# Attention heads taken in pairs: transposed together, scored as 64-row products, gated together

## What is computed

```python
h = jnp.einsum('bnd,de->bne', x, w_in)
qa, ka, va, ga, qb, kb, vb, gb = jnp.split(h, IN_SPLITS, axis=-1)
qa, ka = _rope(qa), _rope(ka)                        # 8 heads of 64
out_a = _dilated_attention(qa, ka, va) * silu(ga)
qb = _axial_rope(_rms_norm_heads(qb, q_norm))        # 8 query heads
kb = _axial_rope(_rms_norm_heads(kb, k_norm))        # 2 key and value heads
out_b = _gqa_attention(qb, kb, vb) * silu(gb)
f = concat(out_a, out_b) @ w_out
y = layer_norm(ALPHA * x + f)
```

## Time and profile before

| | us |
|---|---|
| median of 3 runs | 475.74 |
| lowest, highest | 475.21, 476.89 |
| the profiled execution, first to last instruction | 474.6 |
| TensorE busy in it | 438.0 |
| VectorE, ScalarE, GpSimd busy | 301.4, 230.7, 248.1 |

### The profile page before, as it was taken

How to read it: one execution, slowest core, us unless ns; L and a number is a source line. 1 busy time by engine, 2 the same in 40 slices (tenths; PEclk the granted TensorE clock), 3 DMA queues, 4 the chain that set the end, 5 groups by cost and what they waited for, 6 DMA issues and landing times.

```text
span 474.6 us, 8965 instructions
## 1 busy us (share of the span) xinstructions
PE 438.0 (92%) x3292; PEld 413.2 (87%) x3292; DVE 301.4 (64%) x826; ACT 230.7 (49%) x519; POOL 248.1 (52%) x340
## 2 busy tenths in 40 slices
PE   1999979998899999999999999999999789999990
PEld 1999969987799999998899999999888678999990
DVE  1543675339987788664577877855586777433664
ACT  3332113335456565666565565655675876121222
POOL 1126953795554746334346565653543773454664
PEclk9999989999899999999999999999999989999997
DMA  6611212110200101102010010110200136231222
GB/s 237 255 45 52 71 35 74 39 46 23 68 23 23 46 23 36 56 24 66 14 54 23 24 46 24 40 51 23 68 1 23 44 111 245 88 95 42 78 100 89
DMA packets 23291, 30.00 MB, mean 63 GB/s; under 512 B 1872, under 2 KB 19408, under 8 KB 23248
## 3 DMA queue, kind: packets, MB, share of 16 engines
q1 hardware_dynamic: 22816, 29.30, 19.0%
q10 hardware_dynamic: 432, 0.13, 0.1%
HBM read 26.28 MB, written 3.15 MB: 62 GB/s over the span
## 4 chain that ended last, share of the span: by engine, by line
PE 66%; POOL 10%; DVE 10%; issue 7%; ACT 3%; DMA 2%; SPq 1%; ACTq 0%; DVEq 0%; POOLq 0%
PE bank L504 15%; PE bank L505 15%; PE bank L506 15%; PE bank L465 9%; PE bank L593 6%; POOL scr L1062 3%; DVE prob L870 2%; PE bank L551 2%; PE bank L552 2%; DMA h<-x_prompt 2%; DVE tmp_s L796 1%; POOL tanh L1048 1%; ACT prob L707 1%; DVE p_lo L878 1%; POOL w_lo L1032 1%
## 5 line engine op out<-in xcount | busy, mean ns | idle before, releaser
L504 PE MATMUL bank<-w_hi,t_lo 128*128 128x256 f32 x576 | 168.2, 292 | 1.9 <-DVE nmax L870 0.8
L506 PE MATMUL bank<-w_hi,t_hi 128*128 128x256 f32 x576 | 164.0, 285 | 0.0
L505 PE MATMUL bank<-w_lo,t_hi 128*128 128x256 f32 x576 | 163.9, 285 | 0.0
L504 PEld LDWEIGHTS bank<-w_hi,t_lo 128*128 128x128 f32 x576 | 111.5, 194 | 3.1 <-DVE nmax L870 1.0
L505 PEld LDWEIGHTS bank<-w_lo,t_hi 128*128 128x128 f32 x576 | 111.6, 194 | 0.1
L506 PEld LDWEIGHTS bank<-w_hi,t_hi 128*128 128x128 f32 x576 | 111.3, 193 | 0.0
L1032 POOL TENSOR_TENSOR w_lo<-raw,w_hi 128x512 fp32r<-128x512 f32 x52 | 67.2, 1302 | 59.2 <-ACT w_hi L659 59.1
L1113 POOL TENSOR_SCALAR prob<-prob,den 128x512 f32<-128x512 f32 (+1 forms) x96 | 60.5, 635 | 68.6 <-DVE den L899 68.5
L707 ACT ACTIVATE prob<-prob,nmax 128x512 f32<-128x512 f32 (+1 forms) x96 | 62.3, 649 | 54.1 <-DVE nmax L870 53.6
L878 DVE TENSOR_TENSOR p_lo<-bank,p_hi 128x512 fp32r<-128x512 f32 x80 | 54.8, 685 | 3.0 <-ACT p_hi L716 2.2
L659 ACT ACTIVATE w_hi<-raw 128x512 fp32r<-128x512 f32 x62 | 37.6, 622 | 34.6 <-DMA raw<-w_in 17.4
(11 more groups left out here) (97 smaller groups left out, 784.3 us busy)
## 6 DMA issues: line engine op xcount, KB each, us to landing
raw<-w_in SPq DMA_DIRECT2D x50, 256.0 KB, 2.8
raw<-w_out SPq DMA_DIRECT2D x16, 256.0 KB, 2.9
h<-x_prompt SPq DMA_DIRECT2D x7, 512.0 KB, 6.8
h<-x_sample SPq DMA_DIRECT2D x4, 512.0 KB, 9.6
y_prompt<-h SPq DMA_DIRECT2D x8, 256.0 KB, 2.1
y_sample<-h SPq DMA_DIRECT2D x4, 256.0 KB, 2.1
cst<-consts SPq DMA_DIRECT2D x1, 960.0 KB, 9.5
h<-x_prompt SPq DMA_DIRECT2D x2, 256.0 KB, 3.8
```

Source lines behind the costliest of these rows:

```text
L504: nc.tensor.matmul(out, a_lo, b_hi, start=(m == 0), stop=False)
L505: nc.tensor.matmul(out, a_hi, b_lo, start=False, stop=False)
L506: ins = nc.tensor.matmul(out, a_hi, b_hi, start=False, stop=(m == KT - 1))
```

## The change

Two neighbouring heads make a pair, 8 pairs with 5 steps each (w, 40 steps), and v = 2w + s counts the units as before, s being the head of the pair.

- Queries and keys of a pair lie side by side in 128 columns, so a batch transposes both heads at once and head s lands on rows 64s to 64s + 63. hi and lo get tensors of their own (`q_hi`, `q_lo`). `double_keys` and `k_two` go. For B, where both heads of a pair use one key head, the first key batch is copied to both row halves for both key heads (`twice`): four copies and four subtractions.
- Scores of a step are three rounds, lo x hi, hi x lo, hi x hi, and in each round a 64-row product for either head, on its row half, into its own bank.
- `LAG` becomes one step. Both masks of a step come first on VectorE; probability copies and exponentials alternate on ScalarE.
- Sums of the values get a bank for each head; the second is the one that the batches are transposed into, with waits both ways (`mixed` ahead of a batch, `t_lo_done` ahead of the second head's sums). Both heads are multiplied by the gate in one instruction of 128 partitions.
- The first key and value columns and rotation tables share space with the gates, and values of A get two more places in the space of B's queries.
- The schedules of items, splits and early output products are written anew for steps; six instead of four slices of the first output chunk lie inside the loop.

Its core; of the loops only the new lines stand here:

```diff
-LAG = 3
-STEPS = NU + LAG + 1
-BESIDE = ((0, 5), (3, 8), (55, 44), (62, 50), (65, 52), (72, 54))
-SPLIT_STEPS = (73, 75, 77, 79, 80, 81, 82)
-WIDE_AT = {76: ((0, (0, 1)),), 78: ((1, (0, 1)),), 80: ((2, (0, 1)), (0, (2, 3))), 81: ((1, (2, 3)),),
-           82: ((3, (0, 1)), (2, (2, 3))), 83: ((3, (2, 3)),)}
+LAG = 1
+STEPS = NW + LAG + 1
+BESIDE = ((0, 5), (2, 9), (26, 44), (30, 50), (33, 52), (36, 54))
+SPLIT_AT = {37: (4, 5), 38: (6, 7), 39: (0, 1), 40: (2,)}
+WIDE_AT = {38: ((0, (0, 1)), (1, (0, 1))), 39: ((2, (0, 1)), (3, (0, 1))),
+           40: ((0, (2, 3)), (1, (2, 3)), (2, (2, 3)), (3, (2, 3))),
+           41: ((4, (0, 1, 2, 3)), (5, (0, 1, 2, 3)))}
...
+        h_kv = at("h_kv", [P, TILES, 2 * KV_WIDTH], F32, mix_at)
...
+        v_more = at("v_more", [P, 2, TILES, 2 * HEAD_DIM], F32R, queries_b_at)
...
-        acc, s_ps, pt_ps, o_ps, t_ps = bank[0:2], bank[2:4], bank[4:6], bank[6], bank[7]
+        acc, s_ps, pt_ps, o_ps, t_ps = bank[0:2], bank[2:4], bank[4:6], bank[6:8], bank[7]
...
+            def t_batch(b, w=0):
                 n = t_count[b]
                 if n:
                     pe.wait_ge(t_lo_done, n)
+                if sums_before(w):
+                    pe.wait_ge(mixed, sums_before(w))
...
+                if what == "q":
+                    pe.wait_ge(rope_added, chunk_end(ropes, heads_chunk(2 * p, "q")))
+                    pieces = [qs[:, t, qc:qc + P] for t in range(QT)]
+                elif what == "k":
+                    pe.wait_ge(rope_added, chunk_end(ropes, heads_chunk(2 * p, "k")))
+                    pieces = [ks[:, t, kc:kc + P] for t in range(QT)]
                 else:
+                    pieces = [qs[:, QT + t, qc:qc + P] for t in range(ST)]
+                    if p == 0 or p >= PAIRS_B:
+                        pieces += [ks[:, QT + t, kc:kc + P] for t in range(ST)]
                 transpose_batch(t_ps, pieces).then_inc(t_written, 1)
...
-                    nc.tensor.matmul(out[:], q[:, k * P:(k + 1) * P], k_lo[:, kv % 2, 0:SEQ], start=True, stop=False)
-                    ins = nc.tensor.matmul(out[:], q[:, k * P:(k + 1) * P], k_hi[:, kv % 2, 0:SEQ],
-                                           start=False, stop=True)
...
+                if w:
+                    pe.wait_ge(s_masked, 2 * w)
+                blocks = [(k * P, 0, SEQ, 0)] if k < QT else \
+                    [(SEQ + t * P, SEQ, TOK, t * DEC_SEQ) for t in range(ST)]
+                for n, (q0, k0, k1, at) in enumerate(blocks):
+                    for r, (q, key) in enumerate(((q_lo, k_hi), (q_hi, k_lo), (q_hi, k_hi))):
+                        for s in range(2):
+                            rows = slice(HEAD_DIM * s, HEAD_DIM * (s + 1))
+                            ins = nc.tensor.matmul(s_ps[s][:, at:at + k1 - k0], q[rows, p % 2, q0:q0 + P],
+                                                   key[rows, key_slot(p), k0:k1], start=(r == 0), stop=(r == 2))
+                            if r == 2 and n == len(blocks) - 1:
+                                ins.then_inc(s_ready, 1)
...
+                if s:
+                    pe.wait_ge(t_lo_done, batches_through(step))
...
+            for w in range(STEPS):
+                if w < NW:
+                    scores(w)
+                if LAG <= w < NW + LAG:
+                    for s in range(2):
+                        prob_transposes(2 * (w - LAG) + s)
+                for b in steps[w]:
+                    t_batch(b, w)
+                for m, tiles in WIDE_AT.get(w, ()):
                     wide_tile(m, tiles)
+                for item in items_at(w):
                     project(*item)
+                for G in groups_at(w):
+                    for s in range(2):
+                        values(G, s, w)
...
+            def twice(a, z, c0, c1):
+                return [(a, z, slice(HEAD_DIM * kv, HEAD_DIM * (kv + 1)),
+                         of((k_hi, k_lo), kv, c0, c1, slice(HEAD_DIM * s, HEAD_DIM * (s + 1))))
+                        for kv in range(N_KV_B) for s in range(2)]
+            if what == "q":
+                return [(0, SEQ, slice(0, P), of((q_hi, q_lo), p % 2, 0, SEQ))]
+            if what == "k":
+                return twice(0, SEQ, 0, SEQ) if p == 0 else [(0, SEQ, slice(0, P), of((k_hi, k_lo), p % 2, 0, SEQ))]
+            out = [(0, DEC_SEQ, slice(0, P), of((q_hi, q_lo), p % 2, SEQ, TOK))]
+            if p == 0:
+                out += twice(DEC_SEQ, 2 * DEC_SEQ, SEQ, TOK)
...
+            for w in range(STEPS):
+                for s in range(2):
+                    if LAG <= w < NW + LAG:
+                        prob_high(2 * (w - LAG) + s)
+                    if w < NW:
+                        exps(2 * w + s)
+                for b in steps[w]:
                     t_high(b)
+                for n in split_steps.get(w, ()):
+                    split_mixed(n)
+                for c, n in items_at(w):
                     for g in slices_at(c, n):
                         weights_high(g)
                     evacuate(c, n)
+                for G in groups_at(w):
+                    copy_low(G)
...
+            def mix(G):
+                p, k = divmod(G, GROUPS)
+                for s in range(2):
+                    o = o_lo[HEAD_DIM * s:HEAD_DIM * (s + 1), :]
+                    dve.wait_ge(low_copied, 2 * G + s + 1)
+                    ins = nc.vector.tensor_tensor(o, o_ps[s][0:HEAD_DIM, 0:2 * P], o, ALU.add)
+                after(ins)
+                gate = mix_t[:, gate_tile(p), 2 * P * k:2 * P * (k + 1)]
+                nc.vector.tensor_tensor(gate, o_lo[:], gate, ALU.mult).then_inc(mixed, 1)
...
+            for w in range(STEPS):
+                if w < NW:
+                    for s in range(2):
+                        mask_max(2 * w + s)
+                for s in range(2):
+                    if LAG <= w < NW + LAG:
+                        prob_low(2 * (w - LAG) + s)
+                    if w < NW:
+                        invert(2 * w + s)
+                for b in steps[w]:
                     t_low(b)
+                for n in split_steps.get(w, ()):
+                    if split_order[n] < N_HEADS_A // 2:
+                        mixed_low(n)
+                for item in items_at(w):
                     after_projection(*item)
+                for G in groups_at(w):
+                    mix(G)
...
-            double_keys(0)
+            for kv in range(N_KV_B):
+                split_values(kv * HPC)
...
+            for w in range(STEPS):
+                p, k = divmod(w, UNITS)
+                if w < NW:
+                    for s in range(2):
+                        scale(2 * w + s)
+                for n in split_steps.get(w, ()):
+                    if split_order[n] >= N_HEADS_A // 2:
+                        mixed_low(n)
+                for item in items_at(w):
                     beside_projection(*item)
+                if w < NW and p >= PAIRS_B and k in (0, 1):
+                    split_values(2 * p + k)
```

More of the change, by code:

```diff
@@ L404, in groups_at, with unit @@
-        def groups_at(u):
-            v = u - LAG - 1
-            return [group_of(v)] if 0 <= v < NU and (v == NU - 1 or group_of(v + 1) != group_of(v)) else []
-        def mixed_through(j):
-            return GROUPS * (j + 1)
-        def transposed_at(u):
-            return group_of(u) % 2, u % UNITS % 2
+        split_steps = {w: [split_order.index(k) for k in tiles] for w, tiles in SPLIT_AT.items()}
+        def unit(v):
+            w, s = divmod(v, 2)
+            return *divmod(w, UNITS), s
@@ new lines, in group_of, with groups_at, batches_through, sums_before @@
+        def group_of(v):
+            p, k, s = unit(v)
+            return 2 * (GROUPS * p + k // 2) + s
+        def groups_at(w):
+            p, k = divmod(w - LAG, UNITS)
+            return [GROUPS * p + k // 2] if 0 <= w - LAG < NW and (k % 2 or k == QT) else []
+        def batches_through(w):
+            return len(first) + sum(len(steps[n]) for n in range(w + 1))
+        def sums_before(w):
+            return sum(len(groups_at(n)) for n in range(w))
+        def rows_of(v):
+            k = unit(v)[1]
+            return [(k, 0, SEQ)] if k < QT else [(QT + t, t * DEC_SEQ, (t + 1) * DEC_SEQ) for t in range(ST)]
@@ L567, in prob_transposes, with values @@
+            def prob_transposes(v):
+                pe.wait_ge(scaled, v + 1)
+                if v >= 2:
+                    pe.wait_ge(pt_lo_done, v - 1)
+                transpose_batch(pt_ps[v % 2], [prob[:, v % PRING, n * P:(n + 1) * P] for n in range(4)]) \
                     .then_inc(pt_ready, 1)
-            def values(g):
-                j, k = divmod(g, GROUPS)
-                kv = head_columns(j)[4]
+            def values(G, s, step):
+                p, k = divmod(G, GROUPS)
+                kv = head_columns(2 * p + s)[3]
@@ new lines, in t_high, with exps @@
+                if p >= 2:
+                    act.wait_ge(s_ready, 2 * UNITS * (p - 1))
```

(19 more changed lines are left out.)

384 lines of the change are left out of this document (142 added, 242 removed).

## The result

| | before | after |
|---|---|---|
| median of 4 runs each, us | 476.31 | 480.82 |
| lowest, highest | 475.21, 477.66 | 478.36, 481.17 |
| the profiled execution | 474.6 | 479.0 |

The account below looks back on a forecast made before the run. TensorE was taken to bound the full stretch, the chain through the engines the end. TensorE's work -13.0, start +4.4, early waits +1.3, lag +2.3, end -0.6 sum to -5.6 us: 475.7 becomes 470.1 us, range 456 to 485.

Parts of the forecast that it names:

- I take together: Score rounds: two 64-row products on separate row halves overlap, so a prompt step costs 0.70 us, 7.5 us less over 32.
- Rival (b): Score steps: the array empties at each change between 64-row and 128-row products, 13 us more, 483 us; chance 0.06.
- The sample steps: Eight sample score steps: two stationary loads, 0.216 us a round, are not hidden under 256 columns; 2.9 us more.
- Transposes: Query and key transposes on TensorE: 78 instead of 156, at 0.108 us each whatever the width; 8.4 us less.
- The start: Ahead of the first scores: four key copies and subtractions for one, uncovered stalls of 2.5 and 1.9 us; +4.4 us.
- Early waits and the lag: First five steps' waits on VectorE, +1.3 us; probability transposes one step behind the scores, +2.3 us, between 0 and 9.
- The walk: Steps followed one by one with traced durations, to size waits in the first five steps and the time of steps 30 to 41.
- rival (c): Single-item steps: a lag of one step is too short, TensorE waits 9 us more behind GpSimd's low weights, 479 us; chance 0.08.
- The end: Steps 30 to 41: 72.6 us against 75.6, which gives 0.6 us beyond TensorE's own saving of 2.5.
- The middle: From the first scores to the scores of step 30: a forecast difference of -7.0 us.
- Rival (a): Each score step: the row halves run one after the other, 488 us, slower than before; chance 0.15.
- rival (d): Whole run: everything overlaps, weight loads too, and the waits of the start vanish; -17.1 us, 458.6 us; chance 0.13.

Follow-up runs that it names:

- keys by need: Changed kernel with the second key head of B transposed and copied at pair 2's staging instead of at the start: 476.29 us, ratio to before 0.999.

## Why the prediction was wrong, step by step

**The step that failed** is "I take together ... the nearest row shows that an array used in part is no hindrance". Together was right: the rounds are 0.23 apart. What was wrong was to read from the earlier trace rows that a change of form costs nothing. Those rows are products of 128*64 and 128*128 in turn, which differ in the columns; they alternate for free after the change as well. The row halves do not: 0.31 us a step, 12.6 in all, taken away by one experiment and doubled by another. Rival (b) had this mechanism with 13 us and 483 us in all, and the Trainium skill has it (TensorEngine Tiling (Array Packing), Key Properties: a changed tiling mode drains the engine); the runs here agree with it for row halves, with 0.31 us a visit of two changes. The prediction saw the limit ("for rows no run here shows it") and gave it 0.06 all the same. The evidence against the rule was about another direction of the array, so it was no evidence; the chance should have been near that of the forecast. A step gains 0.24 us in its rounds and pays 0.31 for the two changes: a loss of 0.07.

**The sample steps** were mis-sized the other way. The upper bound of 0.216 us for two loads a round was taken as the price: rounds are 0.12 apart. Without the change of form a sample step costs 0.7, not 1.3: 8 x 0.6 = 4.8 us better than put.

**Transposes.** The price held (0.111 against 0.108), and a pair of heads fits it: units 50 to 59 took 324.32 - 284.48 = 39.84 us with eight items, steps 25 to 29 take 332.94 - 294.33 = 38.61 with eight. Those 1.23 us are about 12 transposes less (1.3), a wait of 0.32 us for the doubled keys at 291.48 that is gone, and scores that cost a little more (5 x 0.05 to 0.07).

**The start** was right (4.3 against 4.4) and its mechanism is confirmed: with two copies in place of four 2.9 of the 4.3 us are gone. That it would pass through whole was not right: like for like half of those 2.8 to 2.9 us is left at step 28, and with the other price gone as well nothing of it is left in the time.

**Early waits and the lag.** The walk gave 1.3 and 2.3 us. The waits of the first five steps are 0.70, 1.09, 0.38 and 2.03, together 0.5 more than the 3.7 of the earlier trace rows; from 140 to 330 us there is none. So 3.1 us better than put; rival (c) did not occur, and a lag of two is slower.

**The end** was put at 72.6 us and took 77.0. The change of form has 10 x 0.31 = 3.1 of it; two sample steps (-1.2) and 12 transposes more saved behind step 30 than counted there (-1.3) go the other way: 73.2. The walk took every duration at the full clock, and the one execution with the clock at 0.98 needed just that, 73.2; the 3.8 us that are left go with the clock of 0.91. That the clock would fall further here than before (0.98) was a term that the forecast did not have.

**The middle** has a slip: by step 30's scores the shorter lag has already done 12 value products and 4 transposes that came after unit 60 before, 1.8 us. The walk of the end had that gain, and the middle was not charged for it. Its miss of 5.5 us is 30 x 0.31 = 9.3, less 6 x 0.6 = 3.6 and 3.1 for waits and lag, plus 1.8 for the slip and 1.3 for the 12 transposes that are saved behind step 30 instead: 5.7.

Against the miss of 10.0 us: +12.6 (form), -4.8 (samples), -3.1 (waits and lag), +1.8 (slip), +3.8 (clock of the end): 10.3. The form is the largest term, but the loss against before also needs the others: 78 transposes (-8.4), scores (40 x 0.07 = +2.8), the start (+4.3) and early waits (+0.5) make -0.8, and the 4.4 us measured come about because the end lost some 5 us in waits and clock. That the kernel without the change of form comes to 470.33 us, where 470.1 was forecast, is luck: terms that were too high and terms that were missing cancel there.

Rival (a) fell with the first look at the rounds: the halves overlap. Of rival (d) the overlap of the loads came true; the early waits did not vanish.

## What to carry to other kernels

A packing that makes products shorter also makes them another form: count the visits to the new form and price each, here 0.3 us against the 0.24 that a visit saved, and put many small products into one visit or leave the form alone. A row that shows one kind of mixing free (columns) says nothing on another kind (rows). And a price on TensorE that is certain in the full stretch (0.111 us a transpose, 4.3 us of a later start) still need not reach the end of the run, where other engines and the clock take it up.

## What the runs showed of the hardware

- Products on two row halves, each of 64 rows, run side by side at the pace of one: 0.23 us for 512 columns and 0.12 for 256, loads included; for 512 columns in whichever order they are queued (one execution).
- A visit to the 64-row form costs 0.31 to 0.34 us: some 0.1 ahead of it, in its first round and behind it, and across the change loads are not taken ahead of the stream. Between 128*64 and 128*128 nothing of the kind is seen.
- The same program behind the same waits may be granted the full clock or half of it: 73.2 us at 0.98 and 77.0 at 0.91 from step 30 to the end of the first output chunk. Ahead of the attention the same happens: from 60 to 72 us the clock was 0.86 in the profiled execution of the changed kernel and 1.00 in three others with the same program up to there, where the first batch of transposes came 1.25 to 1.36 us earlier. Ten executions of keys by need lie between 473.6 us (mean clock of the span 0.988) and 478.2 (0.977).
